# Softmax rounds of a hybrid attention kernel: each stick-breaking query group in front of a pair's transposes

## The chip, the cores and the metric

One core of one Trainium2 chip. The metric is device microseconds (us) of one launch. The kernel before took 1044.19 us, the median of 3 runs (1043.96 to 1045.13).

## The reference, cut to what matters

Two layers of an encoder trunk run for 512 prompt tokens and 64 sample tokens (with 256 cached keys). Each layer projects the stream once and then has two attention branches:

```python
proj = x @ w_in + b_in   # q_a k_a v_a g_a | q_b k_b v_b g_b | q_idx k_idx w_idx | r_a r_b
# branch A, stick-breaking, 8 heads of 64: z = q_a k_a^T / 8, strictly causal
log_keep = where(before, log_sigmoid(-z), 0)
later = cumsum(log_keep, reverse) - log_keep
y_a = where(before, exp(log_sigmoid(z) + later), 0) @ v_a
# branch B, 8 query heads on one key/value head: keys chosen by the indexer's top-k
logits = q_b k_b^T / 8 + bias;  p = softmax(where(chosen, logits, -inf));  y_b = p @ v_b
merged = sigmoid(r_a) * ((y_a * silu(g_a)) @ w_proj_a) + sigmoid(r_b) * ((y_b * silu(g_b)) @ w_proj_b)
x = layer_norm(ALPHA * x + merged @ w_out)
```

The change lies where the softmax of branch B and the projection of branch A's queries, `q_a`, are computed side by side.

## The kernel before, in words

Activations lie by feature (128 features on partitions, 576 tokens along the row) in two parts, a rounded one and its rest; weights likewise. So one dense product is three matmuls per 128 input features: rounded by rounded, rounded by rest, rest by rounded. Weights arrive by SyncE in chunks; ScalarE rounds a unit of 128 output columns (`head`, line 964), GpSimd forms its rest (`rest`, line 1751), and semaphores `s_hi`, `s_lo` pass them on.

**The softmax rounds.** For each layer the query tiles of branch B (prompt tiles 3, 2, 1, the sample tile, prompt tile 0) times 4 head pairs make 20 pairs; pair p holds score rows 2p and 2p+1, each 128 (or 64) queries by 512, 384, 256, 320 or 128 keys. The order of TensorE is written out by hand in the loop of lines 869 to 884. Round r = 0 to 10 issues on TensorE:

- `logits(2r)` and `logits(2r+1)` (line 727), into four PSUM banks; in round 10 the first score product of branch A, `stick_z(0)`, instead;
- `weigh_values(2r-4)` and `(2r-3)` (line 758): transposed probabilities times values;
- then for p = 2r and p = 2r+1: `transpose_probs` of the two rows of pair p-2 (line 740), each row into one of two PSUM banks, and `qa_group` p (line 779): two to four of the eight steps of half a query projection of branch A, all in PSUM bank 7.

A half of a query projection (288 of 576 tokens) is finished at p = 1, 4, 7, 10, 13, 16, 19 and 21 (`QA_HALF_AT`), and the next group waits until VectorE has taken bank 7 out (`qa_half`, lines 1568 for the first half, 1574 and 1576 for the second). So in rounds 2, 5 and 8 the group at 2r ends a second half, and the group at 2r+1 waits for VectorE.

Below, Ta and Tb are the transposes of a round's first and second pair, Qa and Qb its two query groups.

**VectorE in round r** (lines 1647 to 1659): `qa_half` if group 2r-1 ended a half; `masked_logits` of rows 4r and 4r+1 (line 1534: adds mask and bias, writes the row into one of six slots, takes the minimum); `yb_out` of round r-2 (line 1557); `masked_logits` of rows 4r+2 and 4r+3; `qa_half` if group 2r ended a half; `normalise` of pairs 2r and 2r+1 (lines 1547, 1551). The six slots bring a wait with them:

```python
if s >= P_SLOTS:                                     # 6; lines 1529 to 1531
    dve.wait_ge(s_pt, L * N_B + s - P_SLOTS + 1)
```

so row 4r+2 waits for the transposes of row 4r-4, the first of Ta, and row 4r+3 for those of row 4r-3.

**ScalarE in round r** (lines 1246 to 1254) takes in turn one `exp_row` (line 1216) of a new row and one `move_probs` (line 1226), which moves transposed probabilities of row 4r-4, 4r-3, 4r-2, 4r-1 out of PSUM: exp 4r, move 4r-4, exp 4r+1, move 4r-4+1, and so on; behind p = 4, 10 and 16 a `head` as well. `weigh_values` of the next round waits for the moves (`s_ptev`), `transpose_probs(s)` for the move of row s-2 and for `normalise` (`s_pn`). **GpSimd** forms mask plus bias of each row (line 1820) and the rests.

Of the kernel before, what the change touches and what calls it, by code (L numbers as in the profile page):

```python
# [84 lines left out]
def act_evacs(u):  # L85

    return sum(1 for k, _ in UNITS[:u] if k not in ("PR", "GA", "GB"))
# [20 lines left out]
QA_GROUPS = [(n, ks) for n in range(8)  # L108
             for ks in (((0, 1, 2, 3), (4, 5, 6, 7)) if n in (0, 7) else ((0, 1, 2), (3, 4, 5), (6, 7)))]
# [37 lines left out]
def build(nc, A, outs):  # L147
# [7 lines left out]
    with ctx:  # L155
# [230 lines left out]
        def unit_views(u):  # L386

            kind, _ = UNITS[u]
            c = CHUNK_OF[u]
            at = u - FIRST_UNIT[c]  # L390
            k8 = raw[c % 2][:, :].rearrange("p (k c) -> p k c", k=8)
            if kind == "WO":
                src = raw[c % 2][:, :].rearrange("p (k c) -> p k c", k=4)[:, 2 * at:2 * at + 2, :]
                j, q = divmod(u - N_WO, 4)
                dst = [(y[:, q, :] if j else x[u % 2][:, :]).rearrange("p (k c) -> p k c", k=2)
                       for x, y in ((w_hi, wo_hi), (w_lo, wo_lo))]
            else:
                cols = HD + NH if kind == "KI" else 128
                src = k8[:, :, 128 * at:128 * at + cols]
                dst = [x[u % 2][:, :].rearrange("p (k c) -> p k c", k=8)[:, :, 0:cols] for x in (w_hi, w_lo)]  # L400
            return src, dst[0], dst[1]
# [82 lines left out]
        def _(pe):  # L484
# [55 lines left out]
            for L in range(DEPTH):  # L540
# [178 lines left out]
                def logits(p):  # L719
                    ti, m = divmod(p, PAIRS)  # L720
                    tt, t0, n, k0, nk, _, _ = tile_of(*BT_ORDER[ti])
                    if p >= 2:
                        pe.wait_ge(s_rm, L * N_B + 2 * p - 2)
                    for i, (q, k) in enumerate(((q_hi, kb_hi), (q_hi, kb_lo), (q_lo, kb_hi))):
                        for hh in range(2):
                            half = slice(64 * hh, 64 * hh + 64)
                            last = mm(ps[0:n, (2 * p + hh) % 4, 0:nk], q[half, m, t0:t0 + n], k[half, k0:k0 + nk],
                                      start=(i == 0), stop=(i == 2))
                            if i == 2:
                                last.then_inc(s_lg, 1)  # L730

                def transpose_probs(s):
                    ti, h = divmod(s, NH)
                    _, _, n, _, nk, _, _ = tile_of(*BT_ORDER[ti])
                    pe.wait_ge(s_pn, L * N_B + s + 1)
                    if s >= 2:
                        pe.wait_ge(s_ptev, L * N_B + s - 1)
                    for b in range((nk + 127) // 128):
                        kn = min(128, nk - 128 * b)
                        last = nc.tensor.transpose(ps[0:kn, 4 + s % 2, n * b:n * b + n],  # L740
                                                   prob[0:n, s % P_SLOTS, 128 * b:128 * b + kn], ident[0:n, 0:n])
                    last.then_inc(s_pt, 1)

                def weigh_values(p):

                    ti, m = divmod(p, PAIRS)
                    kind, i = BT_ORDER[ti]
                    _, _, n, _, nk, _, _ = tile_of(kind, i)
                    pe.wait_ge(s_ptev, L * N_B + 2 * p + 2)
                    if p >= 2 and p % 2 == 0:  # L750
                        pe.wait_ge(s_yb, L * NBP // 2 + p // 2)
                    at = 128 * (p % 2)
                    nb = (nk + 127) // 128
                    for b in range(nb):
                        kn = min(128, nk - 128 * b)
                        tile = {0: 5, 1: 6, 2: 4}[b] if kind == "s" else b
                        for hh in range(2):
                            last = mm(ps[64 * hh:64 * hh + 64, 6, at:at + n], kv_nat[0:kn, tile, HD:2 * HD],  # L758
                                      prob_T[0:kn, (2 * p + hh) % 4, n * b:n * b + n],
                                      start=(b == 0), stop=(b == nb - 1))  # L760
                    last.then_inc(s_pv, 1)

                def qa_group(n, ks):

                    u = N_QA + n // 2
                    if ks[0] == 0:
                        if n % 2 == 0:
                            pe.wait_ge(s_lo, L * NU + u + 2)
                            if n == 0:
                                pe.wait_ge(s_trev, L * N_TR + N_TR - 1)  # L770
                            else:
                                pe.wait_ge(s_ev, L * N_EV + act_evacs(u))
                        else:
                            pe.wait_ge(s_qhev, L * PAIRS + n // 2 + 1)
                    _, hi, lo = unit_views(u)
                    cols = slice(HALF * (n % 2), HALF * (n % 2) + HALF)
                    for k in ks:
                        for i, (a, b) in enumerate(((hi, xT_hi), (hi, xT_lo), (lo, xT_hi))):
                            last = mm(ps[:, 7, 0:HALF], a[:, k, :], b[:, k, cols],  # L779
                                      start=(k == 0 and i == 0), stop=(k == 7 and i == 2))  # L780
                    if ks[-1] == 7:
                        last.then_inc(s_grp if n % 2 else s_qh, 1)

                def stick_z(p):

                    m, c = divmod(p, A_CHUNKS)
                    if c == 0:
                        pe.wait_ge(s_ev, L * N_EV + act_evacs(N_QA + m) + 1)
                    if p == 0:
                        pe.wait_ge(s_rm, L * N_B + N_B - 2)  # L790
                    else:
                        pe.wait_ge(s_zm, L * NP + p)
                    if c == 2:
                        for n in range(2):
                            mm(ps[:, n, 256:256 + S_HALF], q_s[:, m, :, :],
                                      kT_a[:, m, S_HALF * n:S_HALF * n + S_HALF], start=True, stop=True)
                    for i, at, nk in A_TILES[c]:
                        for hh in range(2):
                            half = slice(64 * hh, 64 * hh + 64)
                            last = mm(ps[:, hh, at:at + nk], q_a[half, m, 128 * i:128 * i + 128],  # L800
                                      kT_a[half, m, PAST + DEC:PAST + DEC + nk], start=True, stop=True)
                    last.then_inc(s_z, 1)
# [66 lines left out]
                for r in range(NBP // 2 + 1):  # L869
                    if r < NBP // 2:  # L870
                        logits(2 * r)
                        logits(2 * r + 1)
                    else:
                        stick_z(0)
                    for p in (2 * r, 2 * r + 1):
                        if r >= 2:
                            weigh_values(p - 4)
                    if r == 1:
                        pe.wait_ge(s_trev, L * N_TR + N_TR)
                    for p in (2 * r, 2 * r + 1):  # L880
                        if r >= 1:
                            transpose_probs(2 * p - 4)
                            transpose_probs(2 * p - 3)
                        qa_group(*QA_GROUPS[p])
                stick_z(1)
                weigh_values(NBP - 2)
                weigh_values(NBP - 1)
# [56 lines left out]
        def _(act):  # L944
# [108 lines left out]
            for L in range(DEPTH):  # L1053
# [105 lines left out]
                for s in range(NH * N_IDX):  # L1159
                    _, _, n, _, nk, _, _ = tile_of(*IDX[s // NH])  # L1160
                    act.wait_ge(s_is, L * NH * N_IDX + s + 1)
                    if s >= RELUS:

                        act.wait_ge(s_acc, L * NH * N_IDX + s - RELUS + 1)
                    act_f(relu[0:n, s % RELUS, 0:nk], ps[0:n, 4 + s % 4, 0:nk], ACT.Relu).then_inc(s_relu, 1)
                    if s == 17:
                        evacuate(U[("KV", 0)])
                    if s == 20:
                        head(U[("KV", 0)] + 2)
                    if s == 23:  # L1170
                        keys_hi(U[("KV", 0)], kb_hi, s_kbhi)
# [761 lines left out]
```

## Time and profile before

| | |
|---|---|
| median of 3 runs | 1044.19 us |
| the profiled execution, its time | 1044.97 us |
| its span, first to last instruction | 1043.0 us |
| TensorE, matmuls busy | 1007.2 us, 97% |
| VectorE, ScalarE, GpSimd busy | 59%, 47%, 48% |
| mean granted TensorE clock | 0.994 |
| softmax rounds, first layer | 162.8 to 231.7 us |
| softmax rounds, second layer | 666.9 to 737.2 us |

A line of the trace in order of time gives the start, the busy time, engine, line, operation, and how many instructions it merges; in brackets stands how long the engine was idle just before, and who released it. A matmul's busy time overlaps that of the next one, so steps are read from start to start. The profiled execution is 0.78 us above the median, and 1.97 us longer than its span.

### The profile page before, as it was taken

What the parts mean: (1) busy time and instruction counts of PE and PEld (TensorE: products, weight loads), DVE (VectorE), ACT (ScalarE), POOL (GpSimd) and SP (SyncE); (2) the same over time, 40 slices, a digit from 0 to 9 for tenths busy, and PEclk for the clock granted to TensorE, in tenths of its full rate; (3) what the DMA queues carried; (4) which work ended last, traced back from release to release, by engine and by line L of the source; (5) the groups of instructions that cost most, each with busy time, mean ns of one, the idle gap of its engine ahead of it and who ended that gap; (6) DMA issues with size and microseconds to landing.
All of it is one profiled execution on the core that took longest, in us unless ns stands there. A gap on an engine that the chain in (4) does not pass through costs nothing.

```text
span 1043.0 us, 18737 instructions
## 1 busy us (share of the span) xinstructions
PE 1007.2 (97%) x7590; PEld 922.9 (88%) x7590; DVE 618.9 (59%) x1217; ACT 489.5 (47%) x843; POOL 500.1 (48%) x335
## 2 busy tenths in 40 slices
PE   5999999999999999999999999999999999999996
PEld 5879997888899999998788899887888999999975
DVE  7579996879963101360765899988898310100137
ACT  6564435659866322223125633466788542222220
POOL 2425455635556734536324265555365474544540
PEclk9999999999999999999999999999999999999999
DMA  5722442101121325323235124301111222342312
GB/s 177 229 68 78 163 147 86 35 9 42 57 66 41 123 84 190 96 83 120 66 137 165 41 93 127 127 2 42 41 42 42 82 81 82 103 160 82 116 47 91
DMA packets 70105, 95.44 MB, mean 92 GB/s; under 512 B 4474, under 2 KB 61284, under 8 KB 69380
## 3 DMA queue, kind: packets, MB, share of 16 engines
q1 hardware_dynamic: 66068, 82.68, 24.4%
q0 software_dynamic: 3776, 11.50, 3.3%
q8 instruction: 60, 0.98, 0.4%
q14 instruction: 25, 0.20, 0.1%
q10 hardware_dynamic: 176, 0.07, 0.0%
HBM read 79.47 MB, written 14.78 MB: 90 GB/s over the span
## 4 chain that ended last, share of the span: by engine, by line
PE 76%; DVE 14%; DMA 3%; ACT 2%; issue 2%; POOL 1%; DVEq 0%; SPq 0%; ACTq 0%; POOLq 0%
PE ps L558 35%; PE ps L913 10%; PE ps L864 10%; DVE attn L1516 3%; PE ps L779 3%; DVE top L1513 3%; DMA raw<-in_w_in 3%; PE ps L800 2%; PE ps L839 2%; PE ps L818 2%; PE ps L581 2%; PE ps L758 2%; DVE attn L1489 2%; DVE attn L1551 1%; PE ps L740 1%
## 5 line engine op out<-in xcount | busy, mean ns | idle before, releaser
L1751 POOL TENSOR_TENSOR w_lo<-raw,w_hi 128x1024 fp32r<-128x1024 f32 x115 | 282.1, 2453 | 391.3 <-ACT w_hi L964 370.8
L558 PE MATMUL ps<-xT_hi,w_hi 128*128 128x288 f32 x864 | 256.8, 297 | 0.0
L558 PE MATMUL ps<-xT_hi,w_lo 128*128 128x288 f32 x864 | 255.2, 295 | 0.0
L558 PE MATMUL ps<-xT_lo,w_hi 128*128 128x288 f32 x864 | 255.2, 295 | 0.0
L964 ACT ACTIVATE w_hi<-raw 128x1024 fp32r<-128x1024 f32 (+1 forms) x116 | 121.4, 1047 | 109.2 <-PE ps L558 73.2
L558 PEld LDWEIGHTS ps<-xT_hi,w_hi 128*128 128x128 f32 x864 | 162.8, 188 | 1.3 <-issue 1.1
L1712 DVE TENSOR_TENSOR qy<-qy,ps 128x576 f32<-128x576 f32 x32 | 24.1, 754 | 235.0 <-PE ps L558 235.0
L558 PEld LDWEIGHTS ps<-xT_lo,w_hi 128*128 128x128 f32 x864 | 162.8, 188 | 0.0
L558 PEld LDWEIGHTS ps<-xT_hi,w_lo 128*128 128x128 f32 x864 | 162.8, 188 | 0.0
L1072 ACT ACTIVATE qy<-ps,bias 128x576 f32<-128x576 f32 x33 | 24.6, 744 | 126.1 <-PE ps L558 126.1
L1843 POOL TENSOR_TENSOR attn<-attn 128x1024 f32<-128x1024 f32 (+1 forms) x24 | 54.3, 2261 | 59.1 <-DVE attn L1624 59.1
L864 PE MATMUL ps<-xT_hi,w_hi 128*128 128x288 f32 x256 | 77.8, 304 | 0.0
L558 PE MATMUL ps<-late_y_hi,w_hi 128*128 128x288 f32 x256 | 75.8, 296 | 1.5 <-POOL late_y_lo L1857 1.5
L558 PE MATMUL ps<-late_y_hi,w_lo 128*128 128x288 f32 x256 | 75.7, 296 | 0.0
L558 PE MATMUL ps<-late_y_lo,w_hi 128*128 128x288 f32 x256 | 75.7, 296 | 0.0
L864 PE MATMUL ps<-xT_lo,w_hi 128*128 128x288 f32 x256 | 75.4, 294 | 0.0
L864 PE MATMUL ps<-xT_hi,w_lo 128*128 128x288 f32 x256 | 75.3, 294 | 0.0
L1624 DVE TENSOR_TENSOR_SCAN attn<-attn 128x512 f32<-128x512 f32 (+4 forms) x72 | 70.9, 1038 | 1.9 <-ACT attn L1244 1.8
L1513 DVE MAX8 top<-attn 128x8 f32<-128x512 f32 (+3 forms) x116 | 63.6, 548 | 3.9
L1820 POOL TENSOR_TENSOR attn<-mask,bias_near 128x256 f32<-128x256 bf16 (+2 forms) x80 | 48.6, 622 | 36.1 <-DVE row_min L1534 35.2
L1216 ACT ACTIVATE attn<-attn,row_min 128x512 f32<-128x512 f32 (+4 forms) x80 | 44.7, 558 | 36.5 <-DVE row_min L1534 36.5
L1516 DVE MATCH_REPLACE8 attn<-top,attn 128x512 f32<-128x512 f32 (+3 forms) x116 | 61.4, 530 | 0.0
(226 smaller groups left out, 2330.7 us busy)
## 6 DMA issues: line engine op xcount, KB each, us to landing
raw<-in_w_in SPq DMA_DIRECT2D x44, 1024.0 KB, 5.2
raw<-in_w_out SPq DMA_DIRECT2D x8, 1024.0 KB, 5.0
x_kept<-x_nat SPq DMA_DIRECT2D x2, 2560.0 KB, 11.1
x_nat<-x_kept SPq DMA_DIRECT2D x2, 2560.0 KB, 11.6
raw<-in_w_proj_a SPq DMA_DIRECT2D x8, 512.0 KB, 3.7
raw<-in_w_proj_b SPq DMA_DIRECT2D x8, 512.0 KB, 4.7
x_nat<-in_x_prompt SPq DMA_DIRECT2D x4, 512.0 KB, 5.5
out<-stage POOLq DMA_DIRECT2D x8, 256.0 KB, 4.3
```

Of the source, the lines that this page charges most:

```text
L558: last = mm(out, a, b[:, HALF * half:HALF * (half + 1)], start=(k == 0 and i == 0), stop=(k == n - 1 and i == 2))
L779: last = mm(ps[:, 7, 0:HALF], a[:, k, :], b[:, k, cols], start=(k == 0 and i == 0), stop=(k == 7 and i == 2))
L864: last = mm(ps[:, 4 + n % 2, 0:HALF], a[:, k, :], b[:, k, cols], start=(k == 0 and i == 0), stop=(k == 7 and i == 2))
L913: last = mm(ps[0:nt, bank, :], a[:, 2 * q + k, t0:t0 + nt], b[:, k, :], start=(first and k == 0 and i == 0), stop=(last_k and k == 1 and i ...
L964: act_f(hi, src, ACT.Copy).then_inc(s_hi, 1)
L1216: act_f(prob[0:n, s % P_SLOTS, 0:nk], prob[0:n, s % P_SLOTS, 0:nk], ACT.Exp, bias=row_min[0:n, c], scale=-1.0, accum_out=row_sum[0:n, c]). ...
L1513: v.max(top8[0:n, r % 2, :], acc).then_inc(s_top, 1)
L1516: v.match_replace(acc, top8[0:n, r % 2, :], acc, TAKEN).then_inc(s_top, 1)
L1624: last = v.tensor_tensor_scan(log, log, from_last(past_clamp[:, at:at + n]), 0.0, ALU.add, ALU.add)
L1751: g.tensor_tensor(lo, src, hi.bitcast(f32), ALU.subtract).then_inc(s_lo, 1)
L1820: g.tensor_tensor(mb[:, far:nk], mask[0:n, mk + far:mk + nk], bn, ALU.add).then_inc(s_mb, 1)
L1843: g.tensor_tensor(z, z, sp_slot[p % 3][:, 0:w], ALU.subtract).then_inc(s_lw, 1)
```

## The change

In the inner loop of each round the query group of p is issued in front of the transposes of pair p-2, not behind them. Qa, Ta, Qb, Tb stand where Ta, Qa, Tb, Qb stood. Nothing else changes: the same instructions, waits and operands; the other engines' programs stay as they are.

```diff
                     if r == 1:
                         pe.wait_ge(s_trev, L * N_TR + N_TR)
                     for p in (2 * r, 2 * r + 1):
+                        qa_group(*QA_GROUPS[p])
                         if r >= 1:
                             transpose_probs(2 * p - 4)
                             transpose_probs(2 * p - 3)
-                        qa_group(*QA_GROUPS[p])
                 stick_z(1)
                 weigh_values(NBP - 2)
                 weigh_values(NBP - 1)
```

## Rows read from the trace of the kernel before

**Rows 1.** The page: busy time, share of the span and instructions of each engine.
```profile
PE 1007.2 (97%) x7590; PEld 922.9 (88%) x7590; DVE 618.9 (59%) x1217; ACT 489.5 (47%) x843; POOL 500.1 (48%) x335
```

**Rows 2.** Rounds 1 to 9 by layer, then what follows: stretch, its length, busy (instructions), clock, DMA.
```profile
169.38:226.22 56.84, 52.80 (x535) 45.23 (x533) 46.60 (x148) 35.63 (x119) 28.68 (x42) 1.00 0.13 45
674.81:731.70 56.89, 52.77 (x533) 45.20 (x533) 46.66 (x148) 35.63 (x119) 28.74 (x42) 1.00 0.11 37
226.22:330.00 103.78, 103.78 (x884) 93.17 (x884) 81.50 (x109) 78.70 (x91) 53.06 (x23) 1.00 0.17 52
```

**Rows 3.** TensorE in order of time, round 1: start, us, line, operation, count, [idle <- releaser].
```profile
169.38 1.28 PE L740 MATMUL ps<-ident,attn 128*128 128x128 f32 x8
...
171.43 0.40 PE L779 MATMUL ps<-xT_hi,w_hi 128*128 128x288 f32 x1 [0.76 <-DVE attn L1568]
...
177.66 1.97 PE L758 MATMUL ps<-attn,kv_nat 128*64 128x128 f32 x32
```

**Rows 4.** TensorE in order of time, round 2 and up to round 4's values.
```profile
179.56 1.09 PE L740 MATMUL ps<-ident,attn 128*128 128x128 f32 x8
...
180.40 0.38 PE L779 MATMUL ps<-xT_hi,w_hi 128*128 128x288 f32 x1
...
181.29 0.60 PE L740 MATMUL ps<-ident,attn 128*128 128x128 f32 x4
...
182.68 0.37 PE L779 MATMUL ps<-xT_hi,w_hi 128*128 128x288 f32 x1
...
184.03 0.45 PE L727 MATMUL ps<-kb_hi,q_hi 64*128 64x384 f32 x2
...
185.28 1.97 PE L758 MATMUL ps<-attn,kv_nat 128*64 128x128 f32 x32
...
187.18 0.87 PE L740 MATMUL ps<-ident,attn 128*128 128x128 f32 x6
...
191.94 1.53 PE L758 MATMUL ps<-attn,kv_nat 128*64 128x128 f32 x24
```

**Rows 5.** VectorE in order of time: round 1, round 2, round 8.
```profile
170.86 0.51 DVE L1568 TENSOR_SCALAR attn<-ps,bias_q 128x288 f32<-128x288 f32 x1
...
180.34 0.56 DVE L1534 CUSTOM_DVE_ANT_0 attn<-ps,attn 128x384 f32<-128x384 f32 x1 [0.25 <-PE ps L740]
...
218.96 0.58 DVE L1574 TENSOR_SCALAR attn<-ps,bias_q 64x64 f32<-64x64 f32 x2 [0.56 <-PE ps L779]
```

**Rows 6.** TensorE in order of time, rounds 5 and 8.
```profile
199.63 0.66 PE L740 MATMUL ps<-ident,attn 128*128 128x128 f32 x4
...
202.32 0.37 PE L779 MATMUL ps<-xT_hi,w_hi 128*128 128x288 f32 x1 [0.51 <-DVE attn L1576]
...
204.68 1.09 PE L758 MATMUL ps<-attn,kv_nat 128*64 128x128 f32 x16
...
217.36 0.57 PE L740 MATMUL ps<-ident,attn 64*128 64x64 f32 x6
...
220.15 0.37 PE L779 MATMUL ps<-xT_hi,w_hi 128*128 128x288 f32 x1 [0.73 <-DVE attn L1576]
...
222.32 1.36 PE L758 MATMUL ps<-attn,kv_nat 128*64 128x64 f32 x24
```

**Rows 7.** ScalarE in order of time, rounds 2 and 3.
```profile
180.25 0.60 ACT L1226 ACTIVATE attn<-ps 128x512 f32<-128x512 f32 x1 [1.52 <-PE ps L740]
...
188.20 0.47 ACT L1226 ACTIVATE attn<-ps 128x384 f32<-128x384 f32 x1
...
188.57 0.61 ACT L1216 ACTIVATE attn<-attn,row_min 128x384 f32<-128x384 f32 x1
```

**Rows 8.** TensorE in order of time, round 1 of the second layer.
```profile
673.84 0.40 PE L727 MATMUL ps<-kb_hi,q_lo 64*128 64x512 f32 x2
...
676.95 0.41 PE L779 MATMUL ps<-xT_hi,w_hi 128*128 128x288 f32 x1 [0.76 <-DVE attn L1568]
```

**Rows 9.** Engines from that round's last logits product to its query product.
```profile
674.24:676.95 2.71, 1.29 (x8) 0.84 (x8) 2.67 (x7) 0.00 (x0) 0.95 (x2) 1.00 0.93 354
```
## The prediction

> **What bounds the kernel now.** I read the page first, then the granted clock and busy time by stretch, then the rounds in order of time, engine by engine, and last the waits. TensorE's matmuls are busy in 97% of the span [rows 1], and where they are idle inside a stage the end moves. Rounds 1 to 9 of each layer take 56.9 us, of which TensorE is idle for 4.0 us in the first layer and 4.1 in the second [rows 2]; behind the rounds it is busy for all of 103.78 us. So whatever the rounds lose or win passes to the end unchanged, and the change cannot win more than about 8 us in all. The other engines are not idle beside it: VectorE is busy for 46.6 of the 56.8 us, and each of its steps waits for ScalarE or TensorE. The reader is to see two kinds of gap: in front of a query group, where VectorE has not yet emptied bank 7 (0.76 us in round 1 [rows 3], 0.51 in round 5 and 0.73 in round 8 [rows 6]), and small ones before transposes. None stands in front of Ta from round 2 on: the transposes that the change wants to cover are ready when their turn comes.
>
> **The change part by part.** It adds and removes no instruction, and no DMA moves: in each of rounds 1 to 10 a TensorE block changes places with another. SyncE's and GpSimd's queues are passed by nothing. TensorE's work costs the same; what counts is who waits for Ta, which now comes a query group later, and who waits for Tb, which now ends the round.
>
> *Round 1.* Qa waits for `qa_half` of the first half, which VectorE starts at 170.86 [rows 5] behind both `normalise`; Qa starts at 171.43 [rows 3]. In the old order the transposes at 169.38 stood in that wait. Now the wait is bare, Qa starts at the same time, and Ta follows it. From Qa's start to the values of round 2 was 177.66 - 171.43 = 6.23 us. New: Qa 1.4, then ScalarE's chain, step B below, at 512 columns: 0.7 + 4 x 0.49 + 3 x 0.7 + 0.1 = 4.9 (0.49 and 0.7 are estimates, the 384-column steps scaled by width). 6.3 against 6.2: no change. Bounds: -0.5 (the chain is no longer than TensorE's own work) to +0.8.
>
> *Step A, rounds 2, 5 and 8: Qb behind VectorE.* Qb waits for `qa_half` of the half that Qa just finished. On VectorE `qa_half` stands behind the masked logits of rows 4r+2 and 4r+3, and these wait for Ta (slots). In the old order that chain began with Ta and ran under Ta, Qa and Tb. In round 2: Ta starts at 179.56, VectorE's row 10 starts at 180.34, released by TensorE's transposes [rows 5], and Qb starts at 182.68 [rows 4]: 3.1 us from Ta to Qb, of which about 0.1 is VectorE's wait for the end of Qa. Now Qa is in front of Ta, so between Ta's start and Qb's lie only Ta's own 0.84 us (180.40 - 179.56) and a stall of 3.0 - 0.84 = 2.1 us. Round 5: 202.32 - 199.63 = 2.7, less about 0.15 of such a wait: 2.55; Ta is 0.4 long, stall 2.1. Round 8: 220.15 - 217.36 = 2.8 less the 0.56 us that VectorE waited for Qa [rows 5, 6]: 2.2; Ta 0.5, stall 1.7. What this costs is the new way from Ta to the next values against the old way without Qa (0.89 us, 181.29 - 180.40):
> - round 2, old: 185.28 - 179.56 - 0.89 = 4.8. New: 3.0 + Qb 1.35 (184.03 - 182.68) + from Tb to the values 2.35 (0.7 to the first move, two moves 0.48 each, one exp 0.6, 0.1) = 6.7. Cost 1.9.
> - round 5, old: 204.68 - 199.63 - 0.89 = 4.2. New: 2.55 + 1.35 + 1.6 = 5.5. Cost 1.3.
> - round 8, old: 222.32 - 217.36 - 1.0 = 4.0. New: 2.2 + 1.35 + 1.6 = 5.1. Cost 1.1.
> Together 4.3 us a layer. The lower bound is that Tb's follow-up hides wholly and each stall costs only itself less the old gap (0.2, 0.7, 0.7) and less 0.6 of slack: 2.5. The upper is the bare stalls, 5.9.
>
> *Step B, the other rounds: values behind ScalarE.* `weigh_values` of the next round waits for the move of the round's last row. ScalarE's queue sets it: behind the start of Ta come 4 moves with 3 exps between them. In round 3, 0.37 us a move (188.57 - 188.20) and 0.60 an exp; the first move starts 0.69 us after Ta's start with four blocks (180.25 - 179.56 [rows 4, 7]), about 0.6 with three. Sum: 0.6 + 4 x 0.37 + 3 x 0.60 + 0.1 = 4.0. Old, without Qa's 1.3: 191.94 - 187.18 - 1.3 = 3.5. Qa used to lie inside this chain as cover and now lies in front: cost 0.5 us. The same sum, with steps narrower as the rows are, gives 0.15 in round 4, 0 in round 6, 0.3 in round 7 and 0.1 in round 9; in rounds 7 and 10 Qa also waits about 0.2 us for a `qa_half` that is behind an exp and a `normalise` made late by Tb. Together 1.3 us a layer; bounds 0 (moves early enough) and 2.5 (0.5 in every one of five).
>
> *What else moves.* VectorE's masked rows at a round's start come behind `normalise`, which now waits longer for an exp behind Tb's move; by my times they start up to 0.8 us later against TensorE, and nothing of TensorE waits for them before Ta is through: cost nothing. If that cover goes, logits of the next round wait for their banks, some 0.5 us a round. GpSimd's mask rows follow VectorE and have over 1 us. `head` behind p = 4, 10, 16 finds its group already done and fits into the stall.
>
> Sum: 0 + 4.3 + 1.3 = 5.6 us a layer. The second layer has the same pattern, 4.1 us idle in 56.9 [rows 2] and the same 0.76 in round 1 [rows 8], so 11.2 in two. Against the profiled execution's 1044.97 that is 1056.2; it stood 0.78 above the median, so I predict **1055.4 us**.
>
> **A rule against the row: the clock.** The new stall in round 2 makes a stretch of 3.0 us with only transposes and waiting. The second layer's round 1 already has one: from the last logits product (673.84 + 0.40) to the query product at 676.95 [rows 8] TensorE does transposes alone and is busy for 1.29 of 2.71 us, at a granted clock of 1.00 [rows 9], the level of 2.4 GHz. The Trainium skill, "TensorE: Matmul & The Clock Gate", Part 4, says that transposes don't count as busy for the clock; Part 1 says that idle stretches bring it down to half. The trace shows no fall there, at a slightly shorter stretch.
>
> **The rivals.**
> - *Clock falls.* If the 3 us stretch did bring 1.2 GHz, Qb of rounds 2, 5 and 8 would take 2.7 instead of 1.35 us: 6 x 1.35 = 8.1 more, 1063.5. Against it: [rows 9]. Chance 0.04.
> - *Stalls only partly paid.* The slack behind Tb absorbs steps A and B down to their lower bounds, 2.5 + 0 a layer, or 3: 1049 to 1050. For it: ScalarE has 21 idle us of 57 [rows 2]. Against: that idle time is in front of exps, not behind Ta. Chance 0.13.
> - *Faster.* Qa ends 0.4 to 0.8 us earlier against the start of a round. If VectorE could take `qa_half` at once, Ta would cover it, and the gaps in front of the query groups (0.76, 0.51, 0.73) would close: 2.0 us a layer, 1040.2. It decides at the masked row 4r+2: if that can start before Ta, this is the way it goes. The bracket at 180.34 says that it is released by the transposes [rows 5], and the slot wait in the code says so too. Chance 0.05.
> - *No change.* Steps A and B are paid out of gaps that also close (4.0 us a layer are idle now): within 2.1 us of 1044.2. Chance 0.07.
> - *Worse.* Late masked rows delay the next logits in most rounds, 0.5 each: 4 a layer more, 1063. Chance 0.05.
>
> **How the numbers follow.** My case has 0.66. Its own bounds are, a layer, 3.5 (A 3.5, B 0.5, round 1 -0.5) to 7.5, so 1051.5 to 1059.5. The range reaches down to the partly paid stalls, 1049.5, and up to 1060.5; below and above lie about 0.2. A measurement of this kernel can tell about 0.2%, 2.1 us, from no change. Slower by more than that: 0.66 + 0.13 + 0.04 + 0.05 = 0.88; same 0.07; faster 0.05.
>
> **What would show it.** Right: in rounds 2, 5 and 8 of both layers a bracket of 1.6 to 2.2 us in front of Qb, released by VectorE's line 1576; in round 1 one of 1.5 us or more in front of Qa, released by line 1568; small ones in front of line 758 released by ScalarE's line 1226; rounds 1 to 9 some 62.5 us long, with TensorE idle for about 10; clock 1.00. Wrong: Qb starts within 1 us of Ta's end in round 2, or row 10 on VectorE starts before Ta; or the loss sits in front of the logits.

## The result, and the profile after

The changed kernel takes 1060.78 us, the median of 4 runs (1054.43 to 1063.39), against 1044.66 for the kernel before (1043.96 to 1046.94, 4 runs). The ratio is 1.0146, with a 95% interval of 1.0120 to 1.0172. The forecast was 1055.4 in a range of 1049.5 to 1060.5: the direction is right, the size is short by 5.4 us, and the median lies 0.3 us above the range's upper end. The kernel before was itself 0.47 us slower here than the 1044.19 us that the forecast started from; the ratio applied to 1044.19 gives 1059.4, inside the range.

The four runs are 9 us apart, where those of the kernel before are 3 us apart, and they order themselves by the granted clock:

| time, us | mean granted TensorE clock |
|---|---|
| 1054.43 | 0.993 |
| 1058.66 (the profiled one) | 0.987 |
| 1062.89 | 0.981 |
| 1063.39 | 0.981 |

The page of the changed kernel, the line that answers to [rows 1]:

```profile
PE 1013.4 (96%) x7590; PEld 930.4 (88%) x7590; DVE 609.0 (58%) x1217; ACT 489.7 (46%) x843; POOL 500.0 (47%) x335
```

The same 7590 matmuls are busy for 6.2 us longer than before: work that is the same took longer, which a stall alone doesn't do. The next view has the stretches that answer to [rows 2], from the last logits product of round 1 to round 10, first and second layer, then two stretches of the second layer's rounds 8 and 9, then one behind the rounds (length; busy time of TensorE, of its weight loads, VectorE, ScalarE, GpSimd; clock; DMA):

```profile
169.62:230.79 61.17, 53.40 (x533) 46.58 (x533) 41.35 (x147) 35.48 (x116) 28.73 (x42) 0.97 0.12 41
678.94:745.13 66.19, 57.68 (x533) 50.94 (x533) 41.50 (x148) 35.47 (x116) 29.29 (x43) 0.90 0.10 34
...
734.00:738.00 4.00, 3.73 (x26) 3.48 (x26) 0.87 (x6) 1.93 (x9) 3.12 (x3) 0.58 0.01 4
738.00:742.00 4.00, 4.00 (x35) 3.41 (x34) 1.16 (x7) 0.50 (x3) 0.81 (x2) 0.50 0.00 0
...
240.00:340.00 100.00, 100.00 (x854) 90.93 (x853) 75.05 (x97) 78.03 (x89) 55.76 (x26) 1.00 0.17 54
```

The clock was 1.00 in both layers before. Now it is 0.97 and 0.90 over the rounds, and 0.50, the level of 1.2 GHz, for a whole stretch of round 9. Behind the rounds TensorE is as busy as ever. Nearly all of the loss lies in the rounds. A run's mean clock also holds falls that have nothing to do with them: in the profiled run of the kernel before, whose rounds are at 1.00, it was 0.70 from 16 to 20 us, 0.57 from 96 to 100 and 0.50 from 1040 to 1044.

The brackets in front of TensorE's query products, first layer rounds 1, 2, 5 and 8, in order of time, answer to [rows 3, 4, 6]; the round-1 bracket of the second layer is the last line. Line 1568 or 1576 as the releaser is VectorE taking bank 7 out:

```profile
171.68 0.37 PE L779 MATMUL ps<-xT_hi,w_hi 128*128 128x288 f32 x1 [2.06 <-DVE attn L1568]
183.03 0.37 PE L779 MATMUL ps<-xT_hi,w_hi 128*128 128x288 f32 x1 [1.85 <-DVE attn L1576]
204.29 0.37 PE L779 MATMUL ps<-xT_hi,w_hi 128*128 128x288 f32 x1 [1.80 <-DVE attn L1576]
224.17 0.37 PE L779 MATMUL ps<-xT_hi,w_hi 128*128 128x288 f32 x1 [1.58 <-DVE attn L1576]
...
681.73 0.37 PE L779 MATMUL ps<-xT_hi,w_hi 128*128 128x288 f32 x1 [2.80 <-DVE attn L1568]
```

And VectorE of the changed kernel in round 2, which answers to [rows 5]: masked rows 10 and 11, then the emptying of bank 7.

```profile
180.88 0.56 DVE L1534 CUSTOM_DVE_ANT_0 attn<-ps,attn 128x384 f32<-128x384 f32 x1 [1.10 <-PE ps L740]
...
181.36 0.55 DVE L1534 CUSTOM_DVE_ANT_0 attn<-ps,attn 128x384 f32<-128x384 f32 x1
...
181.84 0.58 DVE L1574 TENSOR_SCALAR attn<-ps,bias_q 64x64 f32<-64x64 f32 x2
182.43 0.45 DVE L1576 TENSOR_SCALAR attn<-ps,bias_q 128x224 f32<-128x224 f32 x1
```

Row 10 waits 1.10 us for the transposes, the emptying is done at about 182.8, and the query product starts at 183.03, 2.88 us after Ta's start at 180.15.

To split the 13.7 us by which the profiled span grew I took the time from the values of one round (first line-758 product) to those of the next:

| round | before | after, first layer | after, second layer |
|---|---|---|---|
| 2 | 7.62 | 9.17 | 10.74 |
| 3 | 6.66 | 6.68 | 6.68 |
| 4 | 6.23 | 6.34 | 6.36 |
| 5 | 6.51 | 8.75 | 7.57 |
| 6 | 5.78 | 5.76 | 5.43 |
| 7 | 5.61 | 5.71 | 5.70 |
| 8 | 6.25 | 6.95 | 8.62 |
| 9 | 4.96 | 5.14 | 7.72 |
| 10 | 5.44 | 5.60 | 5.69 |

Where the two layers differ by over 1 us (rounds 2, 5, 8, 9) the slower one ran at a lowered clock. The smaller of each pair is the order's own cost: 1.55 in round 2, 1.06 in round 5, 0.70 in round 8, and together about 0.2 in the others; up to round 2's values 0.5 are won. That makes 3.0 us a layer, 6 in both. The rest of the 13.7, over 7 us, is the clock. In a round at a lowered clock the same work takes longer: of the two logits products below, the first is from the kernel before and the second from the same place of the changed kernel, behind its round-5 wait.

```profile
203.87 0.30 PE L727 MATMUL ps<-kb_lo,q_hi 64*64 64x320 f32 x2
...
206.82 0.47 PE L727 MATMUL ps<-kb_lo,q_hi 64*64 64x320 f32 x2
```

### The profile page after: what moved, and what is told of

The parts are those of the page before. It is cut to its first block, busy times and chain, and to the rows that moved or that the text cites. A ratio compares the mean times of both kernels' runs of the same rounds, so it can differ in the third digit from the quotient of the medians.

```text
span 1056.7 us, 18737 instructions
## 1 busy us (share of the span) xinstructions
PE 1013.4 (96%) x7590; PEld 930.4 (88%) x7590; DVE 609.0 (58%) x1217; ACT 489.7 (46%) x843; POOL 500.0 (47%) x335
## 4 chain that ended last, share of the span: by engine, by line
PE 78%; DVE 13%; DMA 3%; issue 2%; ACT 2%; POOL 1%; DVEq 0%; SPq 0%; ACTq 0%; POOLq 0%
PE ps L558 35%; PE ps L913 10%; PE ps L864 10%; PE ps L779 5%; DVE attn L1516 3%; DVE top L1513 3%; DMA raw<-in_w_in 3%; PE ps L758 2%; PE ps L839 2%; PE ps L818 2%; PE ps L800 2%; PE ps L581 2%; PE ps L740 2%; DVE attn L1489 2%; PE ps L727 2%
## 5 line engine op out<-in xcount | busy, mean ns | idle before, releaser
L558 PE MATMUL ps<-xT_hi,w_hi 128*128 128x288 f32 x864 | 256.8, 297 | 0.0
L864 PE MATMUL ps<-xT_hi,w_hi 128*128 128x288 f32 x256 | 77.8, 304 | 0.0
L779 PE MATMUL ps<-xT_hi,w_hi 128*128 128x288 f32 x128 | 43.0, 336 | 15.8 <-DVE attn L1576 10.4
```

What stands on the lines that cost most here:

```text
L558: last = mm(out, a, b[:, HALF * half:HALF * (half + 1)], start=(k == 0 and i == 0), stop=(k == n - 1 and i == 2))
L779: last = mm(ps[:, 7, 0:HALF], a[:, k, :], b[:, k, cols], start=(k == 0 and i == 0), stop=(k == 7 and i == 2))
L864: last = mm(ps[:, 4 + n % 2, 0:HALF], a[:, k, :], b[:, k, cols], start=(k == 0 and i == 0), stop=(k == 7 and i == 2))
```

## The experiments

Three theories stood at first. **M**: masked row 4r+2 waits for Ta, so VectorE empties bank 7 late and the second query group of rounds 2, 5 and 8 stalls; falls of the clock come on top. **S**: ScalarE's moves in front of the values lose time in every round. **C**: the clock alone.

**Only rounds 2, 5 and 8 changed.**

```diff
+                        first = r in (2, 5, 8)
+                        if first:
+                            qa_group(*QA_GROUPS[p])
                         if r >= 1:
                             transpose_probs(2 * p - 4)
                             transpose_probs(2 * p - 3)
+                        if not first:
+                            qa_group(*QA_GROUPS[p])
```

> The query group stands in front only in rounds 2, 5 and 8, the rounds in which the second group waits for VectorE to empty bank 7. Theory M (masked row 4r+2 waits for Ta, so bank 7 is emptied late): brackets of 1.85, 1.80 and 1.58 us in front of the second group as in the changed kernel, 3.3 us a layer, so 6 to 7 us over the kernel before, plus about 1.7 us for each fall of the clock. Rival S (the loss is ScalarE's moves in front of the values, in every round): 1 to 2 us over the kernel before.

Measured: 1060.20 us (1058.27 to 1062.98), ratio 1.0151 (1.0137 to 1.0166), clock 0.982 to 0.987. The brackets in rounds 2, 5 and 8 are 1.85, 1.80 and 1.58 us, as in the changed kernel. These three rounds carry the whole loss, the clock's part included (in the profiled run round 2 takes 10.74 us in both layers).

**All rounds but 1, 2, 5 and 8 changed.** The same edit with `first = r not in (1, 2, 5, 8)`.

> The group stands in front in all rounds but 1, 2, 5 and 8. Theory M: within 1.5 us of the kernel before, TensorE idle in the rounds as before (4.0 us a layer) or less, clock not lower than before. Rival S: 2.5 us or more slower, with brackets in front of the values (line 758).

Measured: 1045.45 us, ratio 1.0007 (0.9999 to 1.0016), clock 0.994 in the profiled run. From its round 2's values to those after round 10 the first layer takes 55.3 us (177.31 to 232.62) against 55.1 before. Where no query group waits for VectorE, the order is worth nothing either way that a median can tell. Theory S falls: six rounds changed, and none takes over 0.2 us more than before.

**The second group behind Tb in rounds 2, 5 and 8** (Qa, Ta, Tb, Qb; `first = p not in (5, 11, 17)`).

> The changed kernel, but in rounds 2, 5 and 8 the second query group stays behind the second pair's transposes (Qa, Ta, Tb, Qb). Theory M: the stall shrinks by Tb's length to about 1.1 us in each; 2 to 4 us over the kernel before. If the clock falls need the long stretch with transposes and waiting only, there are fewer of them or none. Rival S: no better than the changed kernel, 8 us or more over the kernel before.

Measured: 1051.11 us (1048.64 to 1056.19), ratio 1.0072 (1.0050 to 1.0093). The stall splits up. TensorE in order of time, round 2, then the second group of round 5 (line numbers are a few higher here):

```profile
181.08 0.63 PE L740 MATMUL ps<-ident,attn 128*128 128x128 f32 x4 [0.34 <-ACT attn L1230]
182.16 0.63 PE L740 MATMUL ps<-ident,attn 128*128 128x128 f32 x4 [0.46 <-ACT attn L1230]
...
202.96 0.37 PE L779 MATMUL ps<-xT_hi,w_hi 128*128 128x288 f32 x1 [0.28 <-DVE attn L1580]
```

With Tb as cover the wait for VectorE is 0.28 us in round 5 and shows no bracket in round 2, but Ta and Tb now stand side by side and each of Tb's transposes waits for a move out of its bank. The median is 6.5 us over before, more than the 2 to 4 expected. The lowest run, 1048.64, had a clock of 0.997, and the highest, 1056.19, one of 0.984: round 1's bare wait is still there, and in the profiled run the clock fell behind it in the second layer (2.81 us of waiting, then 0.67 from 678 to 682).

**Eight slots in place of six, order as changed.** Rows 6 and 7 go to the staging buffer, whose stores are waited for.

```diff
-P_SLOTS = 6
+P_SLOTS = 8
...
+            return prob[:, c, :] if c < 6 else prob_more[:, c - 6, :]
```

> The changed kernel with 8 probability slots in place of 6 (two of them in the staging buffer), so that masked row 4r+2 waits for transposes of the round before and not for Ta. Theory M: in rounds 2, 5 and 8 the bracket in front of the second group falls to 0.4 to 0.8 us, round 1 keeps its 2.06 us; the time is 1042 to 1046. Rival S: the time stays 6 us or more over the kernel before. Rival C (the loss is only the clock): brackets unchanged.

Measured: 1048.09 us (1047.55 to 1050.43), ratio 1.0040 (1.0028 to 1.0052). Nearly 13 of the 16 us are gone, though the slots alone give nothing (next kernel): that masked row 4r+2 waits for Ta makes most of the stalls. It is 2 us above the expected range. The brackets are 0.98, 1.23 and 0.99 us, not 0.4 to 0.8, and in the profiled run the clock fell behind the 2.80 us wait of the second layer's round 1 (0.63 from 678 to 682 us), which cost 1.5 us up to round 2's values. VectorE in round 2 of this kernel shows what is late next (line numbers are a few higher: 1565 is `yb_out`, 1542 a masked row, 1582 and 1584 the emptying):

```profile
178.63 0.43 DVE L1565 COPY qy<-ps 128x256 f32<-128x256 f32 x1
179.12 0.56 DVE L1542 CUSTOM_DVE_ANT_0 attn<-ps,attn 128x384 f32<-128x384 f32 x1
...
179.76 0.56 DVE L1542 CUSTOM_DVE_ANT_0 attn<-ps,attn 128x384 f32<-128x384 f32 x1
...
180.24 0.58 DVE L1582 TENSOR_SCALAR attn<-ps,bias_q 64x64 f32<-64x64 f32 x2
180.84 0.45 DVE L1584 TENSOR_SCALAR attn<-ps,bias_q 128x224 f32<-128x224 f32 x1
```

VectorE goes through these steps with hardly a pause: it is its queue that is late now, in which both masked rows stand between `yb_out` and the emptying.

**Eight slots, order of before.**

> The kernel before with 8 probability slots and the old order. In the old order VectorE's masked row 4r+2 starts right behind Ta; with 8 slots it need not wait for it, so bank 7 is emptied a little earlier: the 0.51 and 0.73 us in front of the second group in rounds 5 and 8 shrink or stay. 1043 to 1045, the kernel before within 1.5 us. If it were 3 us or more faster, the slots and not the order would be what the rounds wait for.

Measured: 1043.99 us, ratio 0.9997 (0.9988 to 1.0006). The same as before, with the same brackets of 0.51 and 0.73 us: in the old order the slots cost nothing.

**Matmuls in the stall.** In the changed kernel, in front of the query groups p = 2, 5, 11 and 17, 14 matmuls go into a bank that is free just then.

```diff
+                def fill(times, bank, rows_read):
+                    if rows_read:
+                        pe.wait_ge(s_rm, rows_read)
+                    for n in range(times):
+                        mm(ps[:, bank, 0:256], xT_hi[:, n % 8, 0:128], xT_hi[:, n % 8, 0:256], start=True, stop=True)
...
+                        if p in (2, 5, 11, 17):
+                            fill(14, 4 if p == 2 else 0, 0 if p == 2 else L * N_B + 4 * r + 1)
                         qa_group(*QA_GROUPS[p])
```

> The changed kernel with 14 matmuls of 256 columns, whose results nobody reads, in front of the query group in each of the four long waits (rounds 1, 2, 5, 8). They take about 1.5 us of a wait of 1.6 to 2.1. Theory M with the clock (stalls cost 6 to 7 us, the rest of the loss is falls of the clock): no falls in the rounds, 1050 to 1053, runs close together. Rival (the falls have nothing to do with the stalls, or the spread is something else): 1058 to 1063 and spread as in the changed kernel.

Measured: 1051.83 us (1050.96 to 1053.92), ratio 1.0077 (1.0063 to 1.0091), clock 0.994 to 0.998 in all five runs. TensorE does more work and its query groups start no earlier (round 2 takes 9.16 us from values to values, where the changed kernel took 9.17 at full clock), and yet the kernel is about 9 us faster than the changed one. Engines over the rounds of each layer:

```profile
165.00:240.00 75.00, 74.09 (x707) 65.22 (x705) 52.43 (x168) 45.56 (x137) 35.60 (x49) 1.00 0.14 46
670.00:750.00 80.00, 77.80 (x729) 67.55 (x729) 58.04 (x183) 49.15 (x142) 37.44 (x49) 1.00 0.14 45
```

**Transposes in the stall**, 15 of `ident` in place of the matmuls.

```diff
-                        mm(ps[:, bank, 0:256], xT_hi[:, n % 8, 0:128], xT_hi[:, n % 8, 0:256], start=True, stop=True)
+                        nc.tensor.transpose(ps[:, bank, 0:128], ident, ident)
```

> The same as e6_fill, but with 15 transposes of the identity in place of the matmuls, about 1.5 us too. If transposes keep the clock as matmuls do: as e6_fill, 1050 to 1053, close together. If the chip does not count transposes: falls in the rounds and a spread as in the changed kernel, 1055 to 1063.

Measured: 1051.02 us (1050.36 to 1053.23), ratio 1.0069 (1.0056 to 1.0082), clock 0.994 to 0.999. The same two stretches of its profiled run are at 1.00 as well:

```profile
165.00:240.00 75.00, 73.93 (x710) 64.51 (x707) 52.93 (x169) 45.54 (x137) 36.92 (x49) 1.00 0.14 45
670.00:750.00 80.00, 77.46 (x733) 67.15 (x732) 57.98 (x185) 48.45 (x141) 37.45 (x49) 1.00 0.13 43
```

In these waits, transposes kept the clock as well as the matmuls did. With matmuls the kernel is 7.6 us over the kernel before and with transposes 6.8: the order's own cost, near the 6 from the table. The rest of the changed kernel's 16.1 us, 8.5 to 9.4, is what the clock adds at the median. The changed kernel was not timed beside these two; what ties them is the kernel before, 1044.26 us here and 1044.66 there.

**Eight slots, old order in round 1, second group behind Tb.** `first = p not in (2, 3, 5, 11, 17)`.

> 8 slots; old order in round 1; Qa, Ta, Tb, Qb in rounds 2, 5 and 8; the group in front elsewhere. Theory M: in rounds 5 and 8 nothing waits in front of the second group, round 1 as before: 1 to 2 us faster than the kernel before, 1042 to 1043.5, clock as before. Rival S (ScalarE's moves and exps set the rounds): no faster than the kernel before.

Measured: 1047.19 us (1046.29 to 1050.24), ratio 1.0032 (1.0019 to 1.0045): a miss. No query group waits for VectorE in rounds 2, 5 and 8, but Tb does for ScalarE's moves. TensorE, rounds 2, 5 and 8, the first transposes of Tb's first row (each has a like one behind it):

```profile
180.61 0.63 PE L745 MATMUL ps<-ident,stage 128*128 128x128 f32 x4 [0.34 <-ACT attn L1235]
...
201.03 0.41 PE L745 MATMUL ps<-ident,attn 128*128 128x128 f32 x2 [0.35 <-ACT attn L1235]
...
218.81 0.36 PE L745 MATMUL ps<-ident,stage 64*128 64x64 f32 x3 [0.38 <-ACT attn L1237]
```

A query group between Ta and Tb covers the move out of the two transpose banks; taken from there it is missed. From round 2's values on, the first layer takes 56.2 us against 55.1. The second layer also lost 1.5 us in round 8 to the clock, though its waits are short there: in time order, a query product in front of Ta, the longest wait, and a query product behind Tb.

```profile
724.26 0.29 PE L784 MATMUL ps<-xT_hi,w_lo 128*128 128x288 f32 x1
...
725.43 0.36 PE L745 MATMUL ps<-ident,stage 64*128 64x64 f32 x3 [0.38 <-ACT attn L1237]
...
727.47 0.44 PE L784 MATMUL ps<-xT_lo,w_hi 128*128 128x288 f32 x1
```

The granted clock is 0.80 from 724 to 728 us and 0.77 from 728 to 732. So a fall doesn't need a bare wait of 1.5 us; what brought this one stays open.

**VectorE empties bank 7 first**, in the changed kernel with six slots.

```diff
                     if r >= 2:
                         yb_out(r - 2)
+                    if 2 * r in QA_HALF_AT:
+                        qa_half(QA_HALF_AT[2 * r])
                     masked_logits(4 * r + 2)
                     masked_logits(4 * r + 3)
-                    if 2 * r in QA_HALF_AT:
-                        qa_half(QA_HALF_AT[2 * r])
```

> The changed kernel (6 slots), but on VectorE the emptying of bank 7 in rounds 2, 5 and 8 stands in front of masked rows 4r+2 and 4r+3. If the loss is where bank 7's emptying stands in VectorE's queue, the brackets of 1.85, 1.80 and 1.58 us fall to 0.4, 0.8 and 0.7, 2 to 3 us a layer come back, and the clock falls less often: 1044 to 1049, round 1 keeping its 2.06 us. Rival (the transposes' place alone costs it, whatever VectorE does): above 1052.

Measured: 1046.78 us (1044.33 to 1048.85, 12 runs), ratio 1.0018 (1.0008 to 1.0029). 14 of the 16 us are back with TensorE's order untouched. TensorE, first layer, rounds 1, 2, 5 and 8:

```profile
170.51 0.37 PE L779 MATMUL ps<-xT_hi,w_hi 128*128 128x288 f32 x1 [2.06 <-DVE attn L1568]
180.37 0.37 PE L779 MATMUL ps<-xT_hi,w_hi 128*128 128x288 f32 x1 [0.36 <-DVE attn L1576]
200.62 0.37 PE L779 MATMUL ps<-xT_hi,w_hi 128*128 128x288 f32 x1 [0.80 <-DVE attn L1576]
218.29 0.37 PE L779 MATMUL ps<-xT_hi,w_hi 128*128 128x288 f32 x1 [0.73 <-DVE attn L1576]
```

The brackets are those expected to 0.04 us. The rounds of its first layer take 55.4 us from values to values against 55.1 before, and round 1 gives 0.5 back, so without the clock it equals the kernel before. Its runs have 0.990 to 0.996 where those of before mostly have 0.994; round 1's bare wait of 2.06 and 2.80 us is left. In the profiled run the clock fell behind the 2.80 us (0.50 from 676 to 680 us), and up to round 2's values that layer took 2.3 us longer than the changed kernel, in whose profiled run the same wait brought no fall.

**The same on VectorE in the order of before**, and the first half emptied between the two `normalise` of round 0 (line 1658).

> The order of before, with VectorE's queue changed: bank 7 is emptied in front of masked rows 4r+2 and 4r+3 in rounds 2, 5 and 8, and of the first half between the two normalise of round 0. The gaps of 0.76, 0.51 and 0.73 us in front of the query groups should close: 1 to 2 us a layer, 1040.5 to 1043. If the masked rows that now come 1.2 us later hold up ScalarE and so the moves, nothing is won: 1044.

Measured: 1047.14 us (1044.62 to 1052.47), ratio 1.0021 (1.0009 to 1.0034): slower, not faster. TensorE, rounds 1, 5 and 8 of the first layer:

```profile
173.00 0.63 PE L740 MATMUL ps<-ident,attn 128*128 128x128 f32 x4 [1.55 <-ACT attn L1226]
...
203.68 0.37 PE L779 MATMUL ps<-xT_hi,w_hi 128*128 128x288 f32 x1 [0.51 <-DVE attn L1576]
...
221.50 0.37 PE L779 MATMUL ps<-xT_hi,w_hi 128*128 128x288 f32 x1 [0.73 <-DVE attn L1576]
```

In rounds 5 and 8 the emptying begins when Qa ends in either queue order; the gap is its own 1.2 us less Tb, and this edit can take nothing off it. In round 1 the 0.76 us in front of Qa and the 0.58 in front of the transposes behind it became one wait of 1.55 us: ScalarE's move was what round 1 waited for. Counted from the last group of line-701 transposes in front of the stage to round 2's values, this made no difference in the second layer (17.0 us, as before); in the first the clock fell behind the wait (0.66 from 173 to 177 us), and it took 17.0 in place of 15.5. Round 3 takes 6.98 us in place of 6.66 in both layers.

**The group in front but for round 1, VectorE as in the kernel above.**

> The group in front in rounds 2 to 10, the old order in round 1, and VectorE's queue as in e10_before_dve. Brackets in front of the second group of rounds 2, 5 and 8 of 0.3 to 0.8 us, about as long as before: 1043 to 1046, and slower than e10_before_dve, since Ta alone (0.4 to 0.84 us) covers an emptying of 1.2 us, where before Ta or Tb did and nothing was won by the order itself.

Measured: 1047.26 us (1044.37 to 1048.61), ratio 1.0018 (1.0008 to 1.0027). The brackets are as expected (0.36, 0.79, 0.73); round 1 has the 1.55 us of the kernel above, and the median is 1 us above the expected range and no slower than that one. No version beat the kernel before; the eight slots in its own order tie with it.

## Why the prediction was right, and where its sum was off

**Direction and mechanism: right.** The step said to decide, that masked row 4r+2 waits for Ta, so that Qb is late in rounds 2, 5 and 8, is shown from three sides: those rounds alone give the whole loss; two more slots take nearly 13 us back; the emptying moved in front of the rows takes 14. The stalls forecast were 2.1, 2.1 and 1.7 us; they are 1.85, 1.80 and 1.58.

**Step A: the mechanism right, the size too high.** The forecast was 1.9 + 1.3 + 1.1 = 4.3 us a layer, and the table has 1.55 + 1.06 + 0.70 = 3.3. The stalls' size is 0.7 of it (5.9 forecast, 5.2 measured); the rest is the way through Qb and from Tb to the values (in round 2, 1.26 and 2.22 us, where the sum had 1.35 and 2.35).

**Step B: wrong.** The forecast was 1.3 us a layer for values that wait for ScalarE's last move. Measured: about 0.2 outside of rounds 2, 5 and 8, and the kernel that changes only other rounds than 1, 2, 5 and 8 is the same as before within 0.2%. The chain of moves was right: in round 3 of the changed kernel it ends as summed, ScalarE's last move starting at 193.15.

```profile
190.22 0.49 ACT L1226 ACTIVATE attn<-ps 128x384 f32<-128x384 f32 x1 [1.41 <-PE ps L740]
...
193.15 0.49 ACT L1226 ACTIVATE attn<-ps 128x384 f32<-128x384 f32 x1
```

But the values began at 193.19, before that move was done. The step let both `weigh_values` of a round wait for the last row of the round before. The kernel has

```python
pe.wait_ge(s_ptev, L * N_B + 2 * p + 2)   # in weigh_values(p)
```

so the first of the two needs only the first pair's rows; the second, 0.7 us later, needs the last. The sign that the step had named, brackets in front of line 758 released by line 1226, shows in no round of the changed kernel.

**Round 1: as forecast**, a bare wait of 2.06 us and no loss by itself; 0.5 us is won, the end that its bound allowed.

**The clock: the step that failed.** The rival had 0.04, 8.1 us and a time of 1063.5; the measured addition is about 9 us at the median, so this rival, on top of a smaller own loss, is what happened. The forecast for rounds 1 to 9 was 62.5 us with TensorE idle for 10, at a clock of 1.00; they took 61.2 and 66.2 us, idle for 7.8 and 8.5, at 0.97 and 0.90. The argument against it was one row [rows 9]: a stretch of 2.71 us with only transposes and waiting, at a clock of 1.00. That showed only that such a stretch doesn't always bring a fall. In the changed kernel there are eight bare waits of 1.6 to 2.8 us, the profiled run fell behind some (round 5 of the first layer, rounds 2 and 8 of the second) and not behind others (the longest, 2.80 us, behind which it did fall with eight slots and with VectorE's emptying in front), and the runs differ among each other. I priced it as all or nothing, and from one case. The Trainium skill, "TensorE: Matmul & The Clock Gate", says in Part 1 that idle stretches bring the clock to half. The runs agree as far as filling the waits ended the falls in the rounds. The same page of the Trainium skill says in Part 4 that transposes don't count as busy in the same way. For these float32 transposes the runs don't bear that out: 15 of them in each wait held the run's mean clock at 0.994 to 0.999, as 14 matmuls did.

**That the forecast fell near the result is luck:** two errors stand against each other. The order's own cost of 6 to 7.6 us was forecast as 11.2, and the clock's 9 or so as nothing. A slip beside them: 3.5 and 7.5 us a layer on 1044.2 give 1051.2 and 1059.2, not 1051.5 and 1059.5.

## What to carry to other kernels

Before moving work on a saturated engine as "cover", follow who is released by the work that it overtakes: here VectorE's next step hung on the overtaken transposes by a ring of slots, and the step behind it on VectorE's queue was the one that the moved work's successor waits for. A bare TensorE wait can cost more than its length: behind waits of 1.55 to 2.81 us the clock fell in some places and runs here and not in others. Look at the granted clock by stretch before explaining a time, since the mean of a run also holds falls elsewhere. Where a wait lay in pieces of 0.5 to 0.8 us, as in the kernel before, its profiled rounds had no fall; one kernel's clock fell behind pieces of 0.3 and 0.4 us, so that is no guarantee. A wait that cannot be removed can be filled with unused matmuls or transposes, which took about 9 us off the changed kernel.

## What the runs showed of the hardware

- A fall of the granted clock in the rounds made the work behind it longer by up to half: round 8 took 8.62 us in place of 6.95, round 9 took 7.72 in place of 5.14. Whether a given wait brings one varies from run to run of one kernel (clock 0.981 to 0.993).
- Transposes of the identity in the waits held the clock of the profiled rounds at 1.00, the level of 2.4 GHz, as matmuls did (1051.02 and 1051.83 us, each within 3 us over five runs, against a spread of 9 us without them).
- VectorE's first `normalise` of round 2 had taken 2.94 us for two instructions beside a rest that GpSimd formed (2.40 us); in the changed kernel, where GpSimd comes later, the same two take 0.75. It lies off TensorE's path, and the time from round 2's values to round 3's grew all the same.
